# Second block of a two-block layer stack: input and output projections computed as three rounded products instead of one full-precision product

## What is computed

```python
h = rmsnorm_2(x, norm_mix_g[l])
uv, z, xbc, dt_raw, c_q, c_kv, k_rope = split_cols(h @ w_in[l])
y_a = gmlp_mixer(uv, ...)              # u and v, 256 columns each
y_b = ssd_mixer(z, xbc, dt_raw, ...)   # gate z 384, channels xbc 640
y_c = mla_mixer(c_q, c_kv, k_rope, ...)  # latents 384 and 256, rotary key
mix = concatenate([y_a, y_b, y_c])
x = x + mix @ w_out[l]
x = x + squared_relu_mlp(rmsnorm_2(x, norm_mlp_g[l]), mlp_w1[l], mlp_w2[l])
```

## Time and profile before

| | us |
|---|---|
| median of 3 runs | 3802.98 |
| lowest and highest | 3800.29, 3806.8 |
| profiled execution: span of its instructions | 3806.2 |
| TensorE busy in it | 3538.5 |
| VectorE busy | 1367.1 |
| ScalarE busy | 1025.2 |

### The profile page before, as it was taken

How to read it: one execution, slowest core, us unless ns; L and a number is a source line. 1 busy time by engine, 2 the same in 40 slices (tenths; PEclk the granted TensorE clock), 3 DMA queues, 4 the chain that set the end, 5 groups by cost and what they waited for, 6 DMA issues and landing times.

```text
span 3806.2 us, 63151 instructions
## 1 busy us (share of the span) xinstructions
PE 3538.5 (93%) x28236; PEld 2192.0 (58%) x28236; DVE 1367.1 (36%) x2462; ACT 1025.2 (27%) x1992; POOL 283.6 (7%) x242
## 2 busy tenths in 40 slices
PE   6989999999899999999778887899999999999998
PEld 4555344334457588888443332356568885647886
DVE  2242001001532267777440000255453435545343
ACT  3130111111342255545210001224232322423131
POOL 0010000000000234443100000000000000000000
PEclk9999999999799999999989999999999999999999
DMA  8246988984334344332429999831133222122320
GB/s 345 78 183 272 370 320 332 362 341 172 130 116 171 89 97 93 74 72 72 158 116 377 421 415 421 354 101 45 45 100 100 89 76 86 45 67 89 97 92 23
DMA packets 340511, 666.47 MB, mean 175 GB/s; under 512 B 156600, under 2 KB 250296, under 8 KB 284944
## 3 DMA queue, kind: packets, MB, share of 16 engines
q1 hardware_dynamic: 330128, 633.14, 46.0%
q10 hardware_dynamic: 6912, 18.88, 1.3%
q0 software_dynamic: 3200, 10.42, 0.8%
HBM read 630.92 MB, written 31.46 MB: 174 GB/s over the span
## 4 chain that ended last, share of the span: by engine, by line
PE 77%; DVE 8%; DMA 7%; ACT 3%; POOL 2%; issue 1%; SPq 0%; DVEq 0%; ACTq 0%; POOLq 0%
PE ps L952 13%; PE ps L957 5%; DMA ring<-in_moe_wu 4%; PE ps L627 4%; PE ps L2970 3%; PE ps L2954 3%; PE ps L2971 3%; PE ps L2953 3%; PE ps L2952 3%; PE ps L2969 3%; PE ps L2569 3%; PE ps L2675 3%; POOL ring L1732 2%; PE ps L2293 2%; PE ps L1360 2%; PE ps L1385 2%
## 5 line engine op out<-in xcount | busy, mean ns | idle before, releaser
L952 PE MATMUL ps<-ring,H 128*64 128x512 f32 x2016 | 483.0, 601 | 36.9 <-DMA ring<-in_moe_wu 32.4
L1061 DVE TENSOR_TENSOR scr<-ps,scr 128x512 f32<-128x512 f32 x32 | 22.1, 692 | 921.7 <-PE ps L957 516.4
L952 PEld LDWEIGHTS ps<-ring,H 128*64 128x64 f32 x2016 | 143.4, 137 | 321.5 <-issue 246.4
L952 PE MATMUL ps<-ring,scr 128*64 128x512 f32 x1016 | 246.3, 603 | 31.6 <-DMA ring<-in_moe_wd 27.9
L2934 DVE TENSOR_TENSOR ring_rounded<-ring,scr_rounded 128x2048 fp32r<-128x2048 f32 x64 | 146.7, 2293 | 218.7 <-ACT scr_rounded L2927 218.3
L2952 PE MATMUL ps<-scr_rounded,ring_rounded 128*128 128x512 f32 x512 | 203.6, 398 | 0.0
L2954 PE MATMUL ps<-scr_rounded 128*128 128x512 f32 x512 | 202.6, 396 | 0.0
L2971 PE MATMUL ps<-scr_rounded 128*128 128x512 f32 x512 | 202.4, 395 | 0.0
L2953 PE MATMUL ps<-H_rounded,scr_rounded 128*128 128x512 f32 x512 | 202.3, 395 | 0.0
L2969 PE MATMUL ps<-scr_rounded,ring_rounded 128*128 128x512 f32 x512 | 201.7, 394 | 0.0
L2927 ACT ACTIVATE scr_rounded<-ring 128x2048 fp32r<-128x2048 f32 x64 | 122.1, 1908 | 244.7 <-PE ps L2971 244.7
(11 more groups left out here) (479 smaller groups left out, 6239.4 us busy)
## 6 DMA issues: line engine op xcount, KB each, us to landing
ring<-in_moe_wu SPq DMA_DIRECT2D x128, 1024.0 KB, 8.5
ring<-in_moe_wd SPq DMA_DIRECT2D x127, 1024.0 KB, 9.2
ring<-in_moe_wg SPq DMA_DIRECT2D x124, 1024.0 KB, 8.3
ring<-in_mlp_w SPq DMA_DIRECT2D x64, 1024.0 KB, 5.4
ring<-in_ada_w SPq DMA_DIRECT2D x48, 1024.0 KB, 11.6
ring<-in_w_in SPq DMA_DIRECT2D x14, 1024.0 KB, 5.2
ring<-in_w_out SPq DMA_DIRECT2D x8, 1024.0 KB, 5.2
st_kka<-scr ACTq DMA_DIRECT2D x16, 384.0 KB, 3.5
```

The costliest lines, as they stand in the source:

```text
L952: ins = pe.matmul(bx[64 * n:64 * n + 64, :], stat_x(k), w[:, k % 4, :], start=k == 0, stop=k == KT - 1)
```

## The change

The products of the latents, channels, values, u, gates and output projection take the three-product form. For this:

- the plan gets an entry without a load behind each of these weights (name + ".hi"), whose slot holds the high part; ScalarE writes it (`split_high`), VectorE writes the low part over the weight (`split_low`). Two further entries, "hh.0" and "hh.1", hold the high part of H from the norm to the last gate tile. Slots are no longer given round the ring but to the entry whose user ends first;
- the norm of n2 splits H tile by tile, as that of n3 does: H itself becomes the low part. ScalarE and VectorE do the split of the first latent weight (and ScalarE's of the second) among the tiles of the norm; the others stand between the instructions of mla, mix and wout;
- H is no longer multiplied by the root. What comes out of PSUM is: channels, u and gates by a product on VectorE into SBUF (TB, UU, SZ), ahead of ScalarE's functions, which read these; values by ScalarE's scale, for which TensorE turns the root to one column per token tile (`rv`);
- the eight tiles that go into the output projection are split into spare columns of X and H and one tile of scratch (`mix_high`) and in place.

```diff
+LASTS = {f"i{l}.hh.{n}": f"i{l}.z.1" for l in range(2) for n in range(2)}
...
+    def split(name, src):
+        plan.append((name, src))
+        plan.append((name + ".hi", None))
...
+        for n in range(2):
+            plan.append((f"i{l}.hh.{n}", None))
+        cols(f"i{l}.cq", w[:, 1542:1926], add=split)
+        split(f"i{l}.ckv", w[:, 1926:2182])
+        split(f"i{l}.kr", a["krcat"][l])
...
+        when = {name: i for i, (name, _) in enumerate(plan)}
+        place, before, taken = {}, {}, [(-1, None)] * NSLOT
+        for name, src in plan:
+            if name in apart:
+                place[name] = (None, tile_shape(name, src))
+                continue
+            s = min(range(NSLOT), key=lambda n: taken[n][0])
+            assert taken[s][0] < when[name], name
+            place[name], before[name] = (s, tile_shape(name, src)), taken[s][1]
+            taken[s] = (when[LASTS.get(name, name)], name)
...
+        def release(name):
+
+            return "wf." + (name[:-3] if name[-3:] == ".hi" else name)
+
+        def slot_free(eng, name):
+
+            if before[name] is not None:
+                if later(eng, release(before[name])):
+                    eng.wait_ge(*at(release(before[name])))
+
+        def split_high(act, name):
+
+            s, (rows, cols) = place[name]
+            n = rows // P * cols
+            if later(act, "w." + name):
+                act.wait_ge(*at("w." + name))
+            slot_free(act, name + ".hi")
+            did("A", act.activation(ring_r[:, place[name + ".hi"][0], 0:n], ring[:, s, 0:n], ACT.Copy).then_inc(scalar_done, 1), "wh." + name)
+
+        def split_low(dve, name):
+
+            s, (rows, cols) = place[name]
+            n = rows // P * cols
+            if later(dve, "wh." + name):
+                dve.wait_ge(*at("wh." + name))
+            did("V", dve.tensor_tensor(ring_r[:, s, 0:n], ring[:, s, 0:n], ring_r[:, place[name + ".hi"][0], 0:n].bitcast(F32),
+                                       ALU.subtract).then_inc(vector_done, 1), "ws." + name)
+
+        def split_weight(pe, name):
+
+            if later(pe, "ws." + name):
+                pe.wait_ge(*at("ws." + name))
+            rows, cols = place[name][1]
+            return [ring_r[:, place[w][0], 0:rows // P * cols].rearrange("p (k c) -> p k c", c=cols) for w in (name + ".hi", name)]
...
+                        if norm[1] == "2":
+                            slot_free(act, f"i{norm[2]}.hh.{m // 4}")
+                        did(A_, act.activation(high_tile(norm, m), H[:, m, 0:TX], ACT.Copy).then_inc(scalar_done, 1), f"{HIGH[norm]}hh{m}")
+                        if m in (4, 5):
+                            if norm[1] == "2":
+                                split_high(act, f"i{norm[2]}.cq.{m - 4}")
+                            else:
+                                high_weights(act, int(norm[2]), m - 4)
...
+        def three(pe, out, w, x, start, stop, rest=None):
+
+            pe.matmul(out, w[1], x[0], start=start, stop=False)
+            pe.matmul(rest or out, w[0], x[1], start=False, stop=False)
+            return pe.matmul(out, w[0], x[0], start=False, stop=stop)
...
                     if norm in HIGH and m == 6:
-                        low_weights(dve, int(norm[2]), 0)
+                        if norm[1] == "2":
+                            split_low(dve, f"i{norm[2]}.cq.0")
+                        else:
+                            low_weights(dve, int(norm[2]), 0)
...
             def latent(nm, m, wname, o):
-                w = weight(pe, wname)
+                w = split_weight(pe, wname)
                 b = bank(pe, f"{t0}{nm}{m}")
                 for k in range(KT):
-                    if later(pe, f"{hk}.u{k}"):
-                        pe.wait_ge(*at(f"{hk}.u{k}"))
-                    ins = pe.matmul(b, w[:, k, o:o + P], H[:, k, 0:TX], start=k == 0, stop=k == KT - 1)
+                    if later(pe, f"{hk}.hl{k}"):
+                        pe.wait_ge(*at(f"{hk}.hl{k}"))
...
+            b = bank(pe, f"{t0}rv")
+            for tt in range(4):
+                ins = pe.matmul(b[:, tt:tt + 1], RMS[0:1, tt * P:tt * P + P], ones[0:1, 0:1], start=True, stop=True)
+            did(T_, ins.then_inc(tensor_done, 1), f"{t0}rv")
...
+            split_high(act, f"{t0}ckv")
...
+                    if nm == "cq" and m == 1:
+                        split_high(act, f"{t0}kr")
...
+            did(A_, act.activation(RMSH, halves(MEAN), ACT.Abs_reciprocal_sqrt).then_inc(scalar_done, 1))
...
+                if h in (2, 5):
+                    split_high(act, f"{t0}xbc.{h // 3}")
...
+            split_high(act, f"{t0}xbc.2")
...
+            split_low(dve, f"{t0}cq.1")
             mean_vector(dve, hk, MEAN, MEAN1)
+            split_low(dve, f"{t0}ckv")
+            split_low(dve, f"{t0}kr")
...
-            for k in range(KT):
-                did(V, dve.tensor_tensor(H[:, k, 0:TX], H[:, k, 0:TX], RMS, ALU.mult).then_inc(vector_done, 1), f"{hk}.h{k}")
...
+                if h == 4:
+                    split_low(dve, f"{t0}xbc.0")
+            split_low(dve, f"{t0}xbc.1")
+            split_low(dve, f"{t0}xbc.2")
...
+        def mix_high(k):
+
+            if k == 4:
+                return halves(S(12288, TX, of=scr_r))
+            t, n = {5: (X_r, 0), 6: (X_r, 1), 7: (X_r, 2), 0: (X_r, 3), 1: (H_r, 0), 2: (H_r, 1), 3: (H_r, 2)}[k]
+            return t[:, 2 * n:2 * n + 2, TX:TA]
...
             def feature(nm, m, n):
-                w = weight(pe, f"{t0}{nm}.{m // 2}")
+                w = split_weight(pe, f"{t0}{nm}.{m // 2}")
                 b = bank(pe, f"{t0}{nm}{m}")
                 for k in range(KT):
-                    if later(pe, f"n2{l}.h{k}"):
-                        pe.wait_ge(*at(f"n2{l}.h{k}"))
-                    ins = pe.matmul(b, w[:, k, (m % 2) * P:(m % 2) * P + P], H[:, k, 0:TX], start=k == 0, stop=k == KT - 1)
+                    ins = three(pe, b, [x[:, k, (m % 2) * P:(m % 2) * P + P] for x in w], (high_tile(f"n2{l}", k), H_r[:, k, 0:TX]), k == 0, k == KT - 1)
...
+                o = slice(tt * P, tt * P + P)
                 for k in range(KT):
-                    ins = pe.matmul(b[:, 0:256], H[:, k, tt * P:tt * P + P], w[:, k, :], start=k == 0, stop=k == KT - 1)
+                    ins = three(pe, b[:, 0:256], (high_tile(f"n2{l}", k)[:, o], H_r[:, k, o]), [x[:, k, :] for x in w], k == 0, k == KT - 1)
...
             def part(m, ks):
-                w = weight(pe, f"{t0}wout.{m // 2}")
+                w = split_weight(pe, f"{t0}wout.{m // 2}")
                 if m not in banks:
                     banks[m] = bank(pe, f"wo{l}.{m}.0")
-                for step in ((f"free.{t0}o23", f"{t0}mixg") if ks is first else (f"{t0}mix",)):
-                    if later(pe, step):
-                        pe.wait_ge(*at(step))
                 for k in ks:
-                    ins = pe.matmul(banks[m], w[:, k, (m % 2) * P:(m % 2) * P + P], MIX[:, k, :], start=k == 5, stop=k == 4)
+                    if later(pe, f"{t0}ml{k}"):
+                        pe.wait_ge(*at(f"{t0}ml{k}"))
+                    b = halves(banks[m])
+                    ins = three(pe, b, [x[:, k, (m % 2) * P:(m % 2) * P + P] for x in w], (mix_high(k), halves(MIX_r[:, k, :])), k == 5, k == 4)
...
+                if m == 2:
+                    split_high(act, f"{t0}v")
+                if m == 4:
+                    split_high(act, f"{t0}u")
...
+                did(V, dve.tensor_tensor(halves(TB[:, m % 2, :]), halves(t), RMSH, ALU.mult).then_inc(vector_done, 1), f"free.{t0}xbc{m}")
+                if m == 2:
+                    split_low(dve, f"{t0}v")
+                if m == 4:
+                    split_low(dve, f"{t0}u")
...
+            gate(0)
+            split_low(dve, f"{t0}wout.0")
+            mix_split_low(dve, l, (5, 6, 7, 0, 1))
...
+            gate(1)
             for m in range(3):
                 y = MIX[:, 2 + m, :]
-                if later(dve, f"free.{t0}z{m}"):
...
+            split_low(dve, f"{t0}wout.2")
+            mix_split_low(dve, l, (2, 3, 4))
+            split_low(dve, f"{t0}wout.3")
...
-                i = turns[name]
-                if i >= NSLOT:
-                    if later(sp, "wf." + in_turn[i - NSLOT]):
-                        sp.wait_ge(*at("wf." + in_turn[i - NSLOT]))
+                i = place[name][0]
```

More of the change, by code:

```diff
@@ L297, in build @@
             (8192, 10240, 12288, 4096, 6144))}
-        turns = {name: i for i, name in enumerate(name for name, _ in plan if name not in apart)}
-        in_turn = {i: name for name, i in turns.items()}
-        place = {name: (turns[name] % NSLOT if name in turns else None, tile_shape(name, src)) for name, src in plan}
+        when = {name: i for i, (name, _) in enumerate(plan)}
[33 more added lines that the diff above has]
+            return [ring_r[:, place[w][0], 0:rows // P * cols].rearrange("p (k c) -> p k c", c=cols) for w in (name + ".hi", name)]
         def weight(pe, name, of=ring):
```

(58 more changed lines are left out.)

64 lines of the change are left out of this document (37 added, 27 removed).

## The result

The changed kernel takes 3760.05 us in the median of four runs (3747.81 to 3766.62); the kernel before, run beside it, 3801.64 us. The ratio is 0.9884, 95% interval 0.9865 to 0.9903. A second comparison gave 3755.95 against 3804.43 us, ratio 0.9876 (0.9858 to 0.9895). The forecast was 3761 us, range 3745 to 3777. The profiled execution took 3766.62 us, and its span is 3764.8 us.

What follows compares the result with a forecast made beforehand. It took TensorE to bound the second block's projections. Terms: -65.2 + 8.6 + 1.6 + 6.6 + 0.9 + 3.2 + 2 = -42.3 us, from the median 3803.0 to 3761 us; range 3745 to 3777.

Steps and rivals of the forecast that it cites:

- The products: Second block's projections: a tile takes 5.60 us in rounded products instead of 6.87; with the values, -65.2 us for both layers.
- Start of layer 0: Latents of layer 0: TensorE starts 4.4 us late and waits again before the third tile, a cost of 8.6 us.
- second wait: Third latent tile of each layer: its weight's subtraction is queued behind GpSimd's constants; 2.3 us in layer 0, 3.1 in layer 1.
- the two ends: Latents: time for GpSimd's constants to land after VectorE's last sum; 8.4 us taken, 11.5 us the other end.
- First MLP and start of layer 1: Weight split late in the MLP, cost 1.6 us; layer 1's latents start 2.8 us late and wait again, cost 6.6 us.
- Queries: Queries to first score maximum: three added subtractions lengthen VectorE's chain, +0.9 us in layer 0 and +3.2 us in layer 1.
- Mixer: Mixer and output projection: nothing beyond TensorE's own work, about 144 us with no idle stretch over 1 us.
- the clock's 2 us: Idle stretches of TensorE: slower products at the lower clock afterwards, 2 us taken once; bounds 0 and four times 3 us.
- The margin of the states: Mixer, product with the carried states: VectorE has the states ready 1 us before it, the narrowest place.
- Late VectorE in the mixer: Rival: VectorE's chain becomes the mixer's bound, states and gated rows late by 8 us a layer; 3777 us, chance 0.15.
- Each idle stretch drops the clock: Rival: the clock falls in each new idle stretch and nothing absorbs it, 12 us instead of 2; 3771 us, chance 0.12.
- Full cover: Rival: the starts do not wait and the constants land early, so all -65.2 us is gained; 3738 us, chance 0.08.

Runs made afterwards that it cites:

- the full output projection: Changed kernel with the output projection of both layers back in full-precision products, its weights and gated rows unsplit: 3779.87 us.
- the fourth: Changed kernel with weight splits put ahead of the residual in the MLP's second half and for layer 1's first latent weights: 3755.28 us.
- the second experiment: Changed kernel with VectorE subtracting the second latent weight's low part before it waits for GpSimd's constants, in both layers: 3755.83 us.
- the third experiment: Changed kernel with the low parts of the second and third channel weight subtracted in the mixer, not before the first score maximum: 3753.29 us.
- the last experiment: Changed kernel with VectorE's two additions for the gated rows done five times, ahead of the carried states: 3770.38 us.
- the first experiment: Changed kernel with the high part of layer 0's first latent weight in a slot free earlier than that of "yh": 3755.82 us.
- the kernel with all four edits: Changed kernel with the edits of the first experiment, the second experiment, the third experiment and the fourth together: 3736.24 us, ratio 0.9821 to the kernel before.

## Why the prediction was right

*The products* did what the sum says. Three rounded products replace one full one at 0.2274 to 0.2333 us each, and the full output projection shows 1.26 us a tile against the 1.27 predicted.

*Start of layer 0.* TensorE idle 4.38 us (4.4 predicted), second wait 1.29 us (2.3). GpSimd's chain took 8.2 us, near the lower of the two ends (8.4 and 11.5). So the choice was right; that the weight traffic that moved away is its reason was argued and not tested. The second wait was shorter since the first tile ran at half clock (granted clock 0.50 from 2504.1 to 2507 us), so TensorE reached the wait later.

*First MLP and start of layer 1.* The wait was 1.57 us (1.6), the idle stretch 2.35 us (2.8), the second wait 1.97 us (3.1), from the same two queues that the walk used; the fourth and the second experiment remove them separately. The stage still lost 1.4 us against the forecast, which the clock of 0.93 more than explains.

*Queries.* The first maximum came 30.5 and 28.8 us after the queries' start and 31.4 and 29.7 us after the latents' end, between which the four small products that turn the root stand; predicted were 31.4 and 29.6 from the queries' start. Those products start the queries 0.9 us later and do not lengthen VectorE's chain: counted from its own first instruction behind the latents, the chain to the maximum grew from 30.50 to 31.35 us in layer 0 and from 26.2 to 29.7 in layer 1, against +0.9 and +3.2 forecast. The term left out was what the idle 4.7 and 3.7 us do to the clock behind them: from the maximum to the mixer 47.3 and 47.2 us instead of 45.2, which the third experiment gives back in layer 0.

*Mixer.* "Only TensorE's own work" was right, shown by windows in which TensorE is busy for the whole length although VectorE's work rose from 72.9 to 100.1 us. The size was off: 140.7 us instead of 144. In layer 1, where the clock is 0.98 on both sides, the last two gate tiles and the eight of the output took 68.5 us before and 55.6 after, so each saves 1.29 us; the two of u save 1.42 each, and the channels with the values 9.3 us together instead of 8.6. The first product of the values shows the largest piece:

```profile
3277.62 0.28 PE L609 MATMUL ps<-ring_rounded,H_rounded 128*128 128x256 f32 x1
```

The 120 rounded products of the channels begin at 3250.33, so they took 27.29 us, 0.2274 each and 5.46 us a tile, where the sum had the first MLP's 0.2333 and 5.60; the channels save 7.0 us instead of 6.3. They took 27.3 us in both layers of three profiles; what makes them faster than those of the MLP was not tried. Most of the rest is that a full product took 6.87 us a tile in the long row, but 7.0 to 7.1 for u and the first gate. Layer 0 had a further 1.5 us to gain, as its clock before was 0.97. This mis-sized term, some 4.5 us in both layers together, is what paid for the clock's 2 us, which were really some 7 by an estimate from the third and second experiments: 2 in each layer's attention and 3 in layer 1's latents. The margin of the states, said to be the narrowest place and 1 us, was 2.0, or 2.4 with VectorE's own wait.

*The number.* The mechanism held term by term, but that the first comparison's median lies 1 us from the forecast is partly luck. Errors of opposite sign met, and the second block became 46.8 us shorter between the two profiles where 42.3 were forecast. The first block, which the forecast took as fixed, scatters by more than that difference; the second comparison's median, 3755.95 us, lies 5 us from the forecast.

*Rivals.* Late VectorE in the mixer would have needed 2.4 us more on that chain, and the last experiment shows its price from there on. "Each idle stretch drops the clock" was half right: see below. Full cover was within reach only with other places in the queues.

## What to carry to other kernels

When work is moved from TensorE to preparation on other engines, cost the products by the distance of their starts, and then look for the few preparations whose slot or place in a queue makes them last: here four places held 20 us of a gain of 65, and each was a question of order, not of engine time. A wait for unrelated loads at the head of an engine's queue delays all that stands behind it; what needs no such load goes ahead. Where an engine already idles for another (VectorE for 3.5 us at the mixer's start), a late preparation cost nothing here.

## What the runs showed that was not expected

The granted clock falls to 0.50 in the mixer although TensorE has no idle stretch there. A window of the changed kernel within it:

```profile
2669.40:2675.80 6.40, 6.40 (x32) 5.42 (x31) 6.27 (x22) 4.94 (x10) 0.00 (x0) 0.50 0.00 1
```

TensorE is busy for all of it. The two mixers of the first experiment, which run the same code:

```profile
2611.54:2755.46 143.92, 143.92 (x736) 115.94 (x734) 100.33 (x182) 68.10 (x89) 1.04 (x2) 0.95 0.32 98
3239.11:3379.85 140.74, 140.74 (x736) 113.49 (x734) 100.05 (x182) 68.11 (x89) 1.04 (x2) 0.98 0.32 101
```

In the profiles before and after the fall begins within, or right behind, the six full-precision products (12 records) that spread the scan's rows (L2697 after) and lasts through transposes and products of 64 rows. Its length varied between executions, and the mixer's length with it: 140.7 us at 0.98, 142.4 at 0.96, 143.9 at 0.95. No edit of the queues predicts which. After idle stretches the same scatter: 2.35 to 2.38 us ahead of layer 1's latents were followed by a stage at 0.93 in the first profile and at 1.00 in the second experiment, while the idle 4.4 us of layer 0 were followed by 0.93 in both. The 1.8 us ahead of layer 1's first turn of the scores were followed by a fall in the third experiment and by none in the kernel with all four edits. The Trainium skill ("TensorE: Matmul & The Clock Gate", "Why this matters for your kernels") advises against idle gaps between bursts; the third experiment agrees, where the fall went with the idle 4.7 us, and the mixer shows a fall without any gap. So the clock is worth 3 us a layer either way, cannot be forecast stage by stage, and a comparison within that needs several runs. What brings on the fall in the mixer was not tried and stays open.
